# A one-core hybrid decoder step: mLSTM's n vectors as rows, layer norm without GpSimd, a moved wait, and the second norm's weight in the scaling

## The reference, cut to what matters

```python
h = rms_norm(x, norm_mix)                       # x * rsqrt(mean(x*x)+eps) * g
proj = h @ w_in                                 # 1024 x 10760, split in 16 parts
o_a  = head_rms_norm(hgrn2(...)) * silu(ga)     # 4 heads, per-feature forget gates
h_b, c_new, n_new, m_new = mlstm(qb, kb, vb, i_pre, log_f, c0, n0, m0)
#   C_t = f C + i v k^T, n_t = f n + i k, h = C q / max(|n.q|, exp(-m))
o_b  = sigmoid(ob) * head_rms_norm(h_b)
o_c  = bc * causal_depthwise_conv(cc * xc, w_short)
o_d  = silu(layer_norm(causal_depthwise_conv(ad * sigmoid(gd), w_conf) + b, ln_g, ln_b))
out  = (sum over the four branches of sigmoid(gate) * (o @ w_branch)) @ w_out
x = x + out
x = x + square(relu(rms_norm(x, norm_mlp) @ w_up)) @ w_down
y = rms_norm(x, norm_final)
```

## Time and profile before

| what | value |
| --- | --- |
| median of the runs | 2310.09 us (2306.09 to 2311.28) |
| profiled execution, its span | 2307.39 us, 2305.4 us |
| TensorE busy | 2265.8 us, 98% of the span |
| VectorE, ScalarE, GpSimd busy | 914.6, 556.6, 864.0 us |
| TensorE's granted clock, mean | 0.996 of full speed |
| DMA moved | 139.00 MB, 60 GB/s |

### The profile page before, as it was taken

How to read it: one execution, slowest core, us unless ns; L and a number is a source line. 1 busy time by engine, 2 the same in 40 slices (tenths; PEclk the granted TensorE clock), 3 DMA queues, 4 the chain that set the end, 5 groups by cost and what they waited for, 6 DMA issues and landing times. The chain is left out here.

```text
span 2305.4 us, 33335 instructions
## 1 busy us (share of the span) xinstructions
PE 2265.8 (98%) x13402; PEld 2146.6 (93%) x13402; DVE 914.6 (40%) x1436; ACT 556.6 (24%) x925; POOL 864.0 (37%) x901
## 2 busy tenths in 40 slices
PE   7999989999999999999999999999999999999998
PEld 7999989999999999999999999889989889898896
DVE  5489854535544443102112123463242332423324
ACT  4333231111232222121121213232212122121132
POOL 3677443333132224242242424443324233242341
PEclk9999999999999999999999999999999999999999
DMA  4211220121136666212112122201111111111112
GB/s 145 55 55 48 70 85 19 57 58 48 39 84 69 95 94 78 85 46 84 38 46 85 46 85 71 70 28 46 46 46 45 45 45 36 45 45 45 45 55 78
DMA packets 176800, 139.00 MB, mean 60 GB/s; under 512 B 14638, under 2 KB 155198, under 8 KB 176675
## 3 DMA queue, kind: packets, MB, share of 16 engines
q1 hardware_dynamic: 174197, 127.83, 22.4%
q0 software_dynamic: 2304, 8.91, 1.0%
q10 hardware_dynamic: 182, 0.60, 0.1%
HBM read 118.95 MB, written 18.73 MB: 60 GB/s over the span
## 5 line engine op out<-in xcount | busy, mean ns | idle before, releaser
L731 PE MATMUL acc<-h_hi,w_hi 128*128 128x368 f32 (+1 forms) x2584 | 855.6, 331 | 12.0 <-POOL w_lo L1505 10.5
L733 PE MATMUL acc<-h_hi,w_lo 128*128 128x368 f32 (+1 forms) x2584 | 848.7, 328 | 0.0
L732 PE MATMUL acc<-h_lo,w_hi 128*128 128x368 f32 (+1 forms) x2584 | 847.8, 328 | 0.0
L1505 POOL TENSOR_TENSOR w_lo<-w_raw,w_hi 128x256 fp32r<-128x256 f32 (+1 forms) x491 | 469.9, 984 | 827.6 <-ACT w_hi L1152 827.5
L731 PEld LDWEIGHTS acc<-h_hi,w_hi 128*128 128x128 f32 x2584 | 488.0, 189 | 18.6 <-POOL w_lo L1505 11.6
L732 PEld LDWEIGHTS acc<-h_lo,w_hi 128*128 128x128 f32 x2584 | 488.2, 189 | 0.3
L733 PEld LDWEIGHTS acc<-h_hi,w_lo 128*128 128x128 f32 x2584 | 487.9, 189 | 0.0
L1152 ACT ACTIVATE w_hi<-w_raw 128x1024 fp32r<-128x1024 f32 (+1 forms) x169 | 176.4, 1044 | 519.0 <-PE acc L733 439.2
L1790 DVE TENSOR_TENSOR x<-acc,x 128x512 f32<-128x512 f32 (+1 forms) x291 | 201.1, 691 | 183.1 <-PE acc L733 175.3
L731 PE MATMUL acc<-w_hi,u_hi 128*128 128x512 f32 x480 | 187.4, 390 | 0.9 <-POOL w_lo L1505 0.9
L732 PE MATMUL acc<-w_lo,u_hi 128*128 128x512 f32 x480 | 187.3, 390 | 0.0
(11 more groups left out here) (391 smaller groups left out, 2732.3 us busy)
## 6 DMA issues: line engine op xcount, KB each, us to landing
w_raw<-in_w_in SPq DMA_DIRECT2D x84, 512.0 KB, 3.9
w_raw<-in_w_up SPq DMA_DIRECT2D x32, 512.0 KB, 4.0
w_raw<-in_w_down SPq DMA_DIRECT2D x32, 512.0 KB, 3.7
b_raw<-branch_outputs POOLq DMA_DIRECT2D x16, 544.0 KB, 7.1
w_raw<-in_w_branch SPq DMA_DIRECT2D x16, 512.0 KB, 3.5
xin<-in_x_prompt SPq DMA_DIRECT2D x8, 512.0 KB, 8.3
x<-in_x_prompt SPq DMA_DIRECT2D x16, 256.0 KB, 5.2
w_raw<-in_w_out SPq DMA_DIRECT2D x8, 512.0 KB, 3.8
```

The source lines that it names most:

```text
L731: pe.matmul(out, lh, rh, start=first, stop=False)
L732: pe.matmul(out, lh, rl, start=False, stop=False)
L733: return pe.matmul(out, ll, rh, start=False, stop=last)
L1505: return pool.tensor_tensor(out, x, y, op)
```

## The change

Line numbers of the changed kernel are a few off (L1512 for L1505, L1787 for L1790).

1. *n as rows.* All n vectors are loaded in one transfer of 32 rows (`n_rows`) during HGRN2 head 1, turned by TensorE in "rows_out", kept in `n_all`; a column copy on VectorE puts a head's n in c0b, behind a new wait for `b_out`. New n go to `n_out` and are turned once after the last head and stored as rows. The column transfers go. `m0` and `keepr` are loaded earlier too.
2. *Layer norm.* GpSimd's scale and shift go. VectorE multiplies by ln_g with the inverse root in one instruction, ScalarE's sigmoid adds ln_b as its bias, VectorE's last product adds it again. The three additions stand at items 22, 24 and 26.
3. *Phase 2.* SyncE no longer signs the phase; GpSimd waits for the two stores itself, one item later ("rows"), behind the split of the next unit.
4. *Start.* VectorE copies the spread weight. The first weight loads stand behind tiles 3 and 5, GpSimd's splits at i = 4 and 7.
5. *Second norm.* norm_mlp comes as a tile of 128 equal rows, `gain_m`, and goes into the scaling. `full1` goes. High and low parts are taken from the turned tile directly, the low part all on VectorE, the scaling ahead of it.

```diff
-           [(23, "sum", 1), (32, "var", 0), (33, "root", 0)] + \
+           [(22, "sum", 1), (24, "sum", 2), (26, "sum", 3), (32, "var", 0), (33, "root", 0)] + \
...
             sp.dma_start(c0b[:, :, 0:P], a["state_mlstm_c"][0, :, h].rearrange("b d v -> d b v")) \
                 .then_inc(sem("c0_in"), 16)
-            sp.dma_start(c0b[:, :, P:P + 1], a["state_mlstm_n"][0, :, h].rearrange("b (d a) -> d b a", a=1)) \
-                .then_inc(sem("c0_in"), 16)
...
-                if i in (2, 4):
+                if i in (3, 5):
                     unit_load(i // 2 - 1)
...
+                elif it == ("rec", "A", "lv3", 1):
+                    sp.dma_start(m0[:, 0:NS], a["state_mlstm_m"][0].rearrange("b h -> h b")).then_inc(sem("m0_in"), 16)
+                    sp.dma_start(keepr[:, :], a["keep"]).then_inc(sem("m0_in"), 16)
+                    sp.dma_start(n_rows[:, :], a["state_mlstm_n"][0].rearrange("b h d -> (b h) d")) \
+                        .then_inc(sem("m0_in"), 16)
...
                         if h == H - 1:
-                            sp.wait_ge(sem("a_stored"), 16 * H)
                             sp.wait_ge(sem("a_states_out"), 32 * H)
-                            phase_end(sp, "sp", 2)
...
+                elif s == "norm" and h == H - 1:
+                    pe.wait_ge(sem("b_cnew"), H)
+                    pe.transpose(pz[0:NS * H + H, 4, 0:P], n_out[:, :], ident).then_inc(sem("n_turned"), 1)
...
-                        act.wait_ge(sem("ln_affine"), t + 1)
+                        act.wait_ge(sem("ln_dve"), FT + 6 + t)
...
-                        act.activation((sg_d, y_c)[t % 2][:, :], y_d[:, t, :], ACT.Sigmoid) \
+                        act.activation((sg_d, y_c)[t % 2][:, :], y_d[:, t, :], ACT.Sigmoid,
+                                       bias=par[:, t, R_LNB:R_LNB + 1]) \
...
-                if i in (3, 6):
+                if i in (4, 7):
                     u = i // 3 - 1
...
-                    elif stage == "scale":
-                        pool.wait_ge(sem("ln_dve"), FT + 6 + t)
-                        pool.tensor_scalar(y_d[:, t, :], y_d[:, t, :], par[:, t, R_LNG:R_LNG + 1],
-                                           par[:, t, R_LNB:R_LNB + 1], ALU.mult, ALU.add) \
-                            .then_inc(sem("ln_affine"), 1)
...
                     phase_end(pool, "pool", it[1])
-                    if it[1] == 2:
-                        pool.wait_ge(sem("phase_sp"), 2)
+                elif it[0] == "rows":
+                        pool.wait_ge(sem("a_stored"), 16 * H)
+                        pool.wait_ge(sem("a_states_out"), 32 * H)
                         pool.memset(rt, 0.0).then_inc(sem("rt_zero"), 1)
...
+                    else:
+                        dve.wait_ge(sem("b_out"), h)
+                    dve.tensor_copy(c0b[:, :, P], n_all[:, h:NS * H:H])
...
-                        tt(full_of(full1, n - 1, hh, ORDER[n - 1]), pz[:, 1 + 2 * ((n - 1) % 2) + hh, :]
-                           .rearrange("p (k n) -> p k n", k=4)[:, :, 0:mm], gain, ALU.mult) \
-                            .then_inc(sem("m_full"), 1)
...
+                    stt(halves(xt1[0:m, n % 2, :]), row(c), rs[0:m, c:c + 1], gain_m[0:m, :, :], ALU.mult, ALU.mult) \
+                        .then_inc(sem("m_scaled"), 1)
```

More of the change, by code:

```diff
@@ L388, in build @@
             cdr = sb(st, "cdr", [H, 16])
-            m0 = sb(st, "m0", [H, 16])
-            sb(st, "pad_b", [P, 112])
+            sb(st, "pad_m0", [H, 16])
+            n_all = sb(st, "n_all", [P, NS * H])
+            n_out = sb(st, "n_out", [P, NS * H + H])
+            sb(st, "pad_b", [P, 40])
             vb = sb(st, "vb", [P, NT + 1, 2, P + 2])
@@ L428, in build @@
             with ExitStack() as norm_only:
-                full1 = sb(norm_only, "full1", [P, 4, 512])
+                gain_m = sb(norm_only, "gain_m", [P, 2, 512])
+                sb(norm_only, "pad_n", [P, 2, 512])
                 xt1 = sb(norm_only, "xt1", [P, 2, D])
@@ L724, in _ @@
             sp.wait_ge(out_sem, n_out[0])
-            sp.wait_ge(sem("b_states_out"), 64 * H)
+            sp.wait_ge(sem("b_states_out"), 32 * H)
         @block.tensor
@@ L1177, in _ @@
             load_params(act, PARAMS[:3])
-            act.wait_ge(sem("gain_spread"), 1)
-            for j in range(2):
-                ins = copy(gain_x[:, j * 512:(j + 1) * 512], pz[:, 3 + j, :])
-            ins.then_inc(sem("gain_ready"), 1)
             for i in range(NT + 4):
@@ L1242, in evac @@
                     if g == 0 and name in ("qa", "qb"):
+                        if idx == 0 and name == "qa":
+                            act.wait_ge(sem("oc_stored"), 16 * FT)
                         if idx >= 2:
@@ L1801, in params_out @@
                 tt(lbt[:, 0, :], lbl, lbl, ALU.subtract).then_inc(sem("lb_diff"), 1)
+            dve.wait_ge(sem("gain_spread"), 1)
+            for j in range(2):
+                ins = dve.tensor_copy(gain_x[:, j * 512:(j + 1) * 512], pz[:, 3 + j, :])
+            link(ins)
             for i in range(NT + 4):
@@ L2309, in _ @@
                     mean_square(n, c).then_inc(sem("m_ms"), 1)
+                    dve.wait_ge(sem("m_rs"), n + 1)
+                    if n == 0:
+                        dve.wait_ge(sem("gfin_in"), 16)
+                    if n >= 2:
+                        dve.wait_ge(sem("m_turned"), 2 * n - 2)
+                    stt(halves(xt1[0:m, n % 2, :]), row(c), rs[0:m, c:c + 1], gain_m[0:m, :, :], ALU.mult, ALU.mult) \
+                        .then_inc(sem("m_scaled"), 1)
                 if n:
                     t0, t1 = TT_[ORDER[n - 1]]
-                    dve.wait_ge(sem("m_hi"), 2 * n)
-                    tt(h_lo[:, 4:8, t0:t1], full_of(full1, n - 1, 1, ORDER[n - 1]),
-                       h_hi[:, 4:8, t0:t1].bitcast(F32), ALU.subtract).then_inc(sem("m_lo_b"), 1)
-                if n <= NT:
-                    dve.wait_ge(sem("m_rs"), n + 1)
-                    if n >= 2:
-                        dve.wait_ge(sem("m_turned"), 2 * n - 2)
-                    dve.tensor_scalar(halves(xt1[0:m, n % 2, :]), row(c), rs[0:m, c:c + 1], None, ALU.mult) \
-                        .then_inc(sem("m_scaled"), 1)
+                    for hh in range(2):
+                        dve.wait_ge(sem("m_hi"), 2 * n + hh - 1)
+                        tt(h_lo[:, 4 * hh:4 * hh + 4, t0:t1], turned_m(n - 1, hh),
+                           h_hi[:, 4 * hh:4 * hh + 4, t0:t1].bitcast(F32), ALU.subtract).then_inc(sem("m_lo"), 1)
                 if n == 5:
```

104 lines of the change are left out of this document (46 added, 58 removed).

## The result

Four executions of the changed kernel took 2284.73, 2285.85, 2284.37 and 2284.51 us, median 2284.62; before, 2310.0 (2306.09 to 2311.28). The ratio is 0.9893, interval 0.9881 to 0.9906. The forecast was 2288 with a range of 2283 to 2298. The profiled execution took 2284.73 us, 22.7 less than that of before, against 20.5 summed.

The account below looks back on a forecast made before the run. TensorE, busy 98% of the span, was taken as the bound, so only its idle and lower-clock time could be won. Six gains summed to 20.5 us, taken from a mean of 2308.7: 2288 us, range 2283 to 2298.

Parts of the forecast that it names:

- A: Layer norm: without GpSimd's scale and shift, TensorE's 4.1 us wait and 2.4 us of clock go; 6.5 us.
- B: Phase 2: split ahead of the clearing removes TensorE's 3.8 us wait and 1.7 us of clock; 5.5 us.
- C: mLSTM between heads 1 and 2: without single-float transfers w_raw lands sooner; 1.9 us wait plus 1.6 clock, 3.5 us.
- D: Start: GpSimd's first split, one place later, no longer delays the inverse root for the fifth scaling; 0.9 us.
- E: Second norm: first wait for xt and last for h_lo go, less a longer scaling; 2.2 us, bounds 1.0 to 3.5.
- F: Layer norm's three additions: spread out, they no longer delay VectorE's evacuation va; 1.9 us, bounds 0.2 to 1.9.
- The slack of A: Layer norm: the unit's low part is ready 1.4 to 3.5 us before TensorE arrives.
- the row chain: Rival at phase 2: next unit up to 1.9 us late, the same again by clock; 2291 to 2293 us, chance 0.13.
- the new waits cost nothing: Claim that the waits added for decays, n_out's turn, GpSimd's stores and gain_m's load cost no time.
- small new stalls: Rival behind the removed pauses: earlier arrivals meet late loads, 5 to 10 us come back; 2294 to 2299 us, chance 0.10.

Follow-up runs that it names:

- e1: Changed kernel with GpSimd again applying the layer norm's scale and shift and VectorE multiplying by the inverse root alone; median 2289.76 us.
- e2: Changed kernel with GpSimd again waiting for the stores and clearing its tiles ahead of the next unit's split at phase 2; median 2292.03 us.
- e5: Changed kernel with the whole part on n undone: n loaded and stored by columns, m0 and keep loaded late; median 2290.50 us.
- e3: Changed kernel plus single-float loads and stores of n columns, side by side in unused tiles and an unused buffer; median 2284.99 us.
- e9: Changed kernel plus single-float loads into c0b's unused column and stores from cnb and cnew columns to an unused buffer; 2288.47 us, one execution.
- e10: Changed kernel plus only the single-float stores from strided columns of wide tiles, without the loads; 2284.97 us, one execution.
- e7: Changed kernel with GpSimd's vzb of head 2 moved behind qzb, so behind VectorE's decays; median 2283.05 us.
- e12: Changed kernel with first weight loads behind tiles 2 and 4 and splits at i = 3 and 6 again; 2284.88 us, one execution.

## Why the prediction was right, and where its steps were off

| step | predicted | between the traces | undone alone |
| --- | --- | --- | --- |
| A layer norm | 6.5 | 6.7 | 5.9 |
| B phase 2 | 5.5 | 5.6 | 6.5 |
| C between heads 1 and 2 | 3.5 | 3.7, less 1.45 | 5.4 |
| D start | 0.9 | 1.5 | 0 for the order |
| E second norm | 2.2 | 3.7 | 3.5 |
| F additions | 1.9 | 2.2 | 1.5 |
| ScalarE's wait moved | not priced | 0.6 | 0.6 |
| sum | 20.5 | 22.5 | |

**A and B** held in mechanism and size. Their waits are fixed (4.1 and 3.8 in both directions); what differs from one execution to the next is the clock behind them: A lost 2.4 before and 1.7 in e1, B 1.7 and 2.7. The slack of A, 1.4 to 3.5 by the sum, was 3.0.

**B's rival, the row chain**, did not come, for a reason that the prediction missed. It said that VectorE's chain "doesn't depend on TensorE's pause". It depends on what filled the pause: GpSimd's split of two units ran beside the scans and stretched them (e2: 4.88 against 3.39 us for eight). Rows of before, then of the changed kernel:

```profile
640.17 4.87 DVE L2086 TENSOR_TENSOR_SCAN kqr<-sqb,m,ktb 4x8 f32<-4x8 f32 x8
...
663.40 2.82 POOL L1505 TENSOR_TENSOR w_lo<-w_raw,w_hi 128x256 fp32r<-128x256 f32 x4 [18.52 <-ACT w_hi L1152]
```
```profile
640.24 0.16 DVE L1787 TENSOR_TENSOR nlast<-nlast,mp 4x16 f32<-4x16 f32 x1
...
646.80 2.82 POOL L1512 TENSOR_TENSOR w_lo<-w_raw,w_hi 128x256 fp32r<-128x256 f32 x4 [14.68 <-ACT w_hi L1160]
```

With the split moved, the chain took 15.2 us (625.25 to 640.40), against 17.1 before (636.21 to 653.28); in e2, with the old order, it takes 17.1 again. The low part behind it took 2.82 us, as it had before at this very place, and not the 3.85 to 5.97 that the sum took from other places. So the unit was ready at 649.6, 3.4 ahead of its product at about 653. The change removed most of its own rival, and the rest was the price of the low part.

**C** came out by its number and fell short in its reason. The landing did fall from 20.1 to 7.4, and e5 gets all of it back. But the step that put it down to the count of single floats, at a fifth or more of an average packet each, is not enough: e3 and e9 have the same count and land at 13 to 16 us, e10 has little over half and lands at 16 to 17, all within the slack. In the 30 us of before, the traces' packet records give a single float 36 ns on average, half of an average packet's 71 and together 5.3 us of each engine's 30; by the prediction's own sum that is under 5 us of the 12.7 that the landing fell. The packets of 512 bytes beside them took 49 ns there and 28 in the changed kernel, so most of the time lies in the neighbours. Why is not shown. What the prediction had right is that bytes don't decide it.

**The new wait.** The prediction held that "the new waits cost nothing". None of the waits that it listed did. The 1.45 us are VectorE's old chain of decays, which the pause of C had hidden: the earlier trace rows show TensorE idle until 796.47, and the chain ran from there on (before):

```profile
796.54 6.59 DVE L1793 SCALAR_TENSOR_TENSOR wb<-wb,cols,con 128x128 f32<-128x128 f32 x9 [0.24 <-DVE vb L1790]
```

Copy and decays take 2.35 + 4.37 us in the changed kernel, hardly more than the decays alone did; with the pause back (e5) or vzb moved (e7) the wait is gone. It is the rival "small new stalls" with one case of 1.45 us, where the rival had 5 to 10 in all. The trace of before had the row that warned: TensorE's own idle time at C was also VectorE's time.

**E** was mis-sized, by 1.5 us. The second wait for xt, at the sample tile, was to stay at 1.2 and is 0.40; the likely reason, not tried by itself, is that the residual's parts come sooner without the two products. The first was worth 1.4 and the last low part 1.4, not 1.0. VectorE's own work shows why there was room (before, then after, of the second norm's stretch: total us, mean ns):

```profile
L1790 DVE TENSOR_TENSOR h_lo<-full,h_hi 128x512 fp32r<-128x512 f32 (+1 forms) x9 | 13.5, 1495 | 6.4 <-ACT h_hi L1152 6.4
L1790 DVE TENSOR_TENSOR full<-pz,nrm 128x512 f32<-128x512 f32 (+1 forms) x18 | 11.1, 657 | 3.8 <-PE pz L1076 2.9 <-DVEq L2293 0.4 <-DVE x L1790 0.2
L2319 DVE TENSOR_SCALAR xt<-x,rs 128x1024 f32<-128x1024 f32 (+1 forms) x9 | 7.6, 849 | 0.7 <-POOL rs L1505 0.7
```
```profile
L1790 DVE SCALAR_TENSOR_TENSOR xt<-x,rs,gain_m 128x1024 f32<-128x1024 f32 (+1 forms) x9 | 11.6, 1284 | 5.9 <-POOL rs L1512 5.9
L1787 DVE TENSOR_TENSOR h_lo<-pz,h_hi 128x512 fp32r<-128x512 f32 (+1 forms) x18 | 11.0, 652 | 2.7 <-ACT h_hi L1160 2.7
```

Half of a low part cost VectorE 1495 ns on average beside GpSimd's other half; now both halves cost it 2 x 652 ns. Taking GpSimd out of the split costs VectorE nothing (13.5 to 11.0 us in all), and 11.1 us of products are gone. That GpSimd's company was the price is not shown, since the source changed too: both inputs of the old half (full, h_hi) lie in SBUF, the engines' common memory, while one of the new one (pz) lies in PSUM, the memory that TensorE writes. The one new pair that ran beside GpSimd's w_lo took no longer than the others:

```profile
1481.95 1.28 DVE L1787 TENSOR_TENSOR h_lo<-pz,h_hi 128x512 fp32r<-128x512 f32 x2
...
1481.91 3.27 POOL L1512 TENSOR_TENSOR w_lo<-w_raw,w_hi 128x256 fp32r<-128x256 f32 x4 [1.20 <-ACT w_hi L1160]
```

The second norm also corrects the prediction on the scaling. It read 1.21 us as the price of the one-source form. That was one of two out of nine that ran beside GpSimd; the others took 0.74 or 0.75 us, and the two-source form 1.28 or 1.29 in all nine, none of them beside more than some 0.1 us of GpSimd's work. So the rule of the Trainium skill ("VectorE: DVE Perf Modes", The perf-mode tier table), that the one-source form in float32 runs at twice the rate, is borne out in kind, at 1.7 times. The change does pay 4.0 us of VectorE's time for it (7.6 to 11.6), less than the 11.1 us of products that went.

**D** failed in its mechanism. The prediction gave the 0.9 us to the inverse root that waited behind the first split; e12 puts that order back and gets 0.0. The 1.5 us between the traces are not explained, so whatever of them is real came by luck.

**F** was 2.2 between the traces and 1.5 undone alone. The line beside it, ScalarE's wait for the store of o_c, stood in the diff and was not priced: 0.6 us.

**The level and the sum.** The forecast of 2288 is 3.4 us above the median. Between the two profiled executions the gain is 22.7 against 20.5, which is 2.2 of them; the other 1.2 come from starting at the mean of the executions of before. That the sum came so near is luck in part: the new wait took 1.45 us back, while E, D, F and the line that was not priced brought 3 us more than summed.

## What to carry to other kernels

Where one engine is busy 98%, list its waits by name, add for each the clock lost behind it, and ask of each what engine used the pause: its work is the next wait (VectorE's decays, 1.45 us), or goes faster once the pause's filler has moved (the scans, 4.9 to 3.4). When one kind of row in the trace has two durations, look at what runs beside each before taking one of them as the price. A part undone alone from the finished kernel can be worth another amount than between the two kernels (5.4 us against 3.7 less 1.45), here because one load took 2.4 us longer, for a reason that stays open.
